# Neighbour attention: values weighed in plain float by halves of 64 columns instead of in high and low parts

## The reference, cut to what matters

```python
s = jnp.concatenate([s_win.reshape(B, NA_HEADS, GRID_W, n_win), s_meta], axis=-1)
p = jax.nn.softmax(s, axis=-1).astype(v.dtype)
p_win = p[..., :n_win].reshape(B, NA_HEADS, GRID_W, win_r, NA_WIN_C)
p_meta = p[..., n_win:]
return (jnp.einsum('bhqrc,brqchd->bqhd', p_win, v_win)
        + jnp.einsum('bhqm,bmhd->bqhd', p_meta, v_meta))
```

## Time and profile before

| | |
|---|---|
| median of 3 runs | 1414.36 us (1412.99 to 1416.44) |
| the profiled execution, its own time | 1412.37 us |
| its span, first to last instruction | 1410.6 us |
| mean granted TensorE clock | 0.982 |
| TensorE / VectorE / ScalarE / GpSimd busy | 1335.9 / 777.8 / 507.1 / 606.6 us |
| the neighbour stage | about 1060 to 1365 us of the span |

### The profile page before, as it was taken

The page is one execution under the profiler, slowest core; times in us unless marked ns, Lnnn a source line. Parts: engine busy times, 40 slices in busy tenths (PEclk is TensorE's granted clock), DMA queues, the critical chain, the costliest instruction groups (busy, mean ns, idle before and its releaser), DMA issues.

```text
span 1410.6 us, 20322 instructions
## 1 busy us (share of the span) xinstructions
PE 1335.9 (95%) x6862; PEld 1076.8 (76%) x6862; DVE 777.8 (55%) x1507; ACT 507.1 (36%) x1066; POOL 606.6 (43%) x367
## 2 busy tenths in 40 slices
PE   7999999998999999999985899999899999999987
PEld 6877777785888888888874677777677888888865
DVE  4237775645556565511142677777425776666761
ACT  3233334213333333200023566666103444444420
POOL 5423332353444444555530444443265555544411
PEclk9999999999999999999997999999899999999999
DMA  6422222232333333333230111111043322222112
GB/s 177 107 66 76 70 65 75 75 90 61 103 89 99 94 89 101 96 102 95 85 105 16 45 46 31 45 30 45 15 130 89 83 68 64 71 71 70 48 33 69
DMA packets 196560, 105.38 MB, mean 75 GB/s; under 512 B 18982, under 2 KB 194444, under 8 KB 196508
## 3 DMA queue, kind: packets, MB, share of 16 engines
q1 hardware_dynamic: 196060, 104.00, 25.8%
q0 software_dynamic: 432, 0.69, 0.3%
q10 hardware_dynamic: 16, 0.00, 0.0%
HBM read 102.57 MB, written 2.10 MB: 74 GB/s over the span
## 4 chain that ended last, share of the span: by engine, by line
PE 81%; DVE 6%; issue 5%; POOL 3%; ACT 3%; DMA 1%; SPq 0%; DVEq 0%; POOLq 0%; ACTq 0%
PE ps L352 19%; PE ps L353 19%; PE ps L354 18%; PE ps L374 9%; PE ps L1237 2%; PE ps L1248 1%; POOL w_low L339 1%; PE ps L1265 1%; PE ps L1267 1%; PE ps L1266 1%; POOL y_low L660 1%; PE ps L898 1%; POOL sq L641 1%; PE ps L920 1%; PE ps L1291 1%
## 5 line engine op out<-in xcount | busy, mean ns | idle before, releaser
L339 POOL TENSOR_TENSOR w_low<-w_raw,w_high 128x1024 fp32r<-128x1024 f32 x183 | 447.8, 2448 | 547.3 <-DVE w_high L334 547.2
L352 PE MATMUL ps<-h_high,w_high 128*128 128x512 f32 x864 | 352.9, 408 | 11.4 <-DVE h_low L475 8.4
L353 PE MATMUL ps<-h_low,w_high 128*128 128x512 f32 x864 | 343.5, 398 | 0.0
L354 PE MATMUL ps<-h_high,w_low 128*128 128x512 f32 x864 | 341.9, 396 | 0.0
L334 DVE CAST w_high<-w_raw 128x1024 fp32r<-128x1024 f32 x183 | 136.9, 749 | 138.0 <-PE ps L354 74.0
L352 PEld LDWEIGHTS ps<-h_high,w_high 128*128 128x128 f32 x864 | 163.3, 189 | 61.6 <-issue 20.5
L354 PEld LDWEIGHTS ps<-h_high,w_low 128*128 128x128 f32 x864 | 163.7, 189 | 37.6
L353 PEld LDWEIGHTS ps<-h_low,w_high 128*128 128x128 f32 x864 | 163.5, 189 | 35.0 <-issue 1.7
L2054 DVE SCALAR_TENSOR_TENSOR z<-ps,cv,z 128x511 f32<-128x511 f32 x44 | 33.0, 750 | 97.8 <-ACT z L1518 97.8
L1518 ACT ACTIVATE z<-ps,cv 128x512 f32<-128x512 f32 x44 | 34.3, 779 | 121.9 <-PE ps L354 121.7
L354 PE MATMUL ps<-m_high,w_low 128*128 128x512 f32 x176 | 69.4, 395 | 0.0
(11 more groups left out here) (338 smaller groups left out, 2508.7 us busy)
## 6 DMA issues: line engine op xcount, KB each, us to landing
w_raw<-in_w_in_dram SPq DMA_DIRECT2D x150, 256.0 KB, 3.2
w_raw<-in_w_up_dram SPq DMA_DIRECT2D x88, 256.0 KB, 3.2
w_raw<-in_w_out_dram SPq DMA_DIRECT2D x44, 256.0 KB, 3.0
w_raw<-in_w_down_dram SPq DMA_DIRECT2D x32, 256.0 KB, 3.0
w_raw<-in_w_down_dram SPq DMA_DIRECT2D x16, 192.0 KB, 2.6
rel<-in_rel_bias_dram SPq DMA_DIRECT2D x8, 384.0 KB, 3.2
x_tok<-in_x_dram SPq DMA_DIRECT2D x4, 512.0 KB, 5.7
w_raw<-in_w_ob_dram SPq DMA_DIRECT2D x8, 256.0 KB, 2.9
```

The source lines that it names most:

```text
L339: pool.tensor_tensor(w_low[:, n % RING, :], w_raw[:, n % RAW, :], w_high[:, n % RING, :].bitcast(F32), ALU.subtract).then_inc(low_made, 1)
L352: pe.matmul(acc, wh, mh, start=first and k == 0, stop=False)
L353: pe.matmul(acc, wh, ml, start=False, stop=False)
L354: done = pe.matmul(acc, wl, mh, start=False, stop=last and k == tiles - 1)
```

## The change

The values and the probabilities of the neighbour stage are kept as plain float (F32) instead of high and low parts. `weigh` does, for each key tile and each head, one plain float matmul with the 64 value columns of that head, which writes 64 of the 128 partitions of bank 4; then one for each head with the 16 meta keys. `turn` transposes the 16 meta columns straight from the probabilities. `probs` divides window and meta columns in one operation per head. `copy_b` is one copy, `gated` one operation with 128 rows. `place_v` on VectorE goes, and ScalarE's second operation in its `place_v` sets the semaphore `nv_ready` that TensorE waits for in its place. ScalarE's `copy_a` writes `np_`; `keep_v` loses its second copy. VectorE's list loses `place_v` in both places. `weigh` waits for ScalarE's copy by name too.

```diff
@@ buffers of the neighbour stage @@
-                nv_high = sb("nv_high", [P, 2, 4, P], F32R, a)
-                nv_low = sb("nv_low", [P, 2, 4, P], F32R, a)
-                nv_meta = sb("nv_meta", [80, 2, P], F32R, a)
-                nvf_meta = sb("nvf_meta", [P, 80], F32, a)
+                nv = sb("nv", [P, 2, 4, P], F32, a)
+                nv_meta = sb("nv_meta", [META, 2, P], F32, a)
...
-                ne_meta = sb("ne_meta", [P, 2, 2, 80], F32, a)
-                np_high = sb("np_high", [P, 3, 2, 2 * P], F32R, a)
-                np_low = sb("np_low", [P, 3, 2, 2 * P], F32R, a)
-                np_meta = sb("np_meta", [80, 2, 2 * P], F32R, a)
+                np_ = sb("np_", [P, 3, 2, 2 * P], F32, a)
+                np_meta = sb("np_meta", [META, 2, 2 * P], F32, a)
@@ GpSimd @@
-            pool.memset(nv_meta[:].bitcast(F32), 0.0).then_inc(s["mv_cleared"], 1)
@@ TensorE: turn @@
                 for h in range(2):
-                    mm = pe.transpose(ps[0:80, 3, (2 + h) * P:(3 + h) * P], ne_meta[:, t % 2, h, :], ident[:])
+                    mm = pe.transpose(ps[0:META, 3, (2 + h) * P:(3 + h) * P],
+                                      ne[:, t % 2, h, NA_META[t]:NA_META[t] + META], ident[:])
@@ TensorE: weigh @@
                 pe.wait_ge(s["t_copied_b"], i * 8 + (4 * c + 2 * p + 2))
+                pe.wait_ge(s["t_copied_a"], i * 8 + (4 * c + 2 * p + 2))
                 if p == 0:
-                    pe.wait_ge(s["nv_low_"], i * 2 + (c + 1))
+                    pe.wait_ge(s["nv_ready"], i * 2 + (c + 1))
...
-                    acc = ps[:, 4, :].rearrange("p (h q) -> p h q", h=2)[:, :, q]
-                    vh, vl = nv_high[:, z_, a + p, :], nv_low[:, z_, a + p, :]
-                    pe.matmul(acc, vh, np_high[:, a, :, q], start=a == p, stop=False)
-                    pe.matmul(acc, vh, np_low[:, a, :, q], start=False, stop=False)
-                    pe.matmul(acc, vl, np_high[:, a, :, q], start=False, stop=False)
-                pe.matmul(ps[:, 4, :], nv_meta[:, z_, :], np_meta[:], start=False, stop=True).then_inc(s["t_summed"], 1)
+                    for h in range(2):
+                        d = slice(h * HD, (h + 1) * HD)
+                        pe.matmul(ps[d, 4, q], nv[:, z_, a + p, d], np_[:, a, h, q], start=a == p, stop=False)
+                for h in range(2):
+                    d = slice(h * HD, (h + 1) * HD)
+                    mm = pe.matmul(ps[d, 4, 0:2 * P], nv_meta[:, z_, d], np_meta[:, h, :], start=False, stop=True)
+                mm.then_inc(s["t_summed"], 1)
@@ TensorE: turn_v @@
-                pe.transpose(ps[0:80, 6, 0:P], nvf_meta[:], ident[:]).then_inc(s["nv_turned"], 1)
+                pe.transpose(ps[0:META, 6, 0:P], nvf[:, 0:META], ident[:]).then_inc(s["nv_turned"], 1)
@@ ScalarE: place_v @@
-                act.activation(nv_high[:, c % 2, :, :], ps[:, 5, :].rearrange("p (a d) -> p a d", d=P), ACT.Copy)
-                for r in (0, 32, 64):
-                    v = act.activation(nv_meta[r:r + META, c % 2, :], ps[r:r + META, 6, 0:P], ACT.Copy)
-                v.then_inc(s["nv_high_"], 1)
+                act.activation(nv[:, c % 2, :, :], ps[:, 5, :].rearrange("p (a d) -> p a d", d=P), ACT.Copy)
+                act.activation(nv_meta[:, c % 2, :], ps[0:META, 6, 0:P], ACT.Copy).then_inc(s["nv_ready"], 1)
@@ VectorE: probs @@
-                    dve.tensor_scalar(ne_meta[:, t % 2, h, :].rearrange("p (r m) -> p r m", m=META),
-                                      five(ne[:, t % 2, h:h + 1, m:m + META]), nm[:, t % 2, 2, h:h + 1], None, ALU.mult)
-                    p = dve.tensor_scalar(ne[:, t % 2, h, k:k + w], ne[:, t % 2, h, k:k + w], nm[:, t % 2, 2, h:h + 1],
+                    p = dve.tensor_scalar(ne[:, t % 2, h, 0:w], ne[:, t % 2, h, 0:w], nm[:, t % 2, 2, h:h + 1],
                                           None, ALU.mult)
@@ VectorE: copy_b @@
-                dve.tensor_copy(np_meta[:, :, q], src).then_inc(s["t_meta"], 1)
-                dve.tensor_tensor(np_low[:, a:a + n, :, q], turned(n), np_high[:, a:a + n, :, q].bitcast(F32), ALU.subtract)
-                dve.wait_ge(s["t_meta"], i * 8 + (4 * c + t + 1))
-                dve.tensor_tensor(np_meta[32:64, :, q], src[32:64], np_meta[32:64, :, q].bitcast(F32), ALU.subtract)\
+                dve.tensor_copy(np_meta[:, :, q], ps[0:META, 3, 2 * P:4 * P].rearrange("p (h q) -> p h q", h=2))\
                     .then_inc(s["t_copied_b"], 1)
@@ VectorE: gated @@
-                for h in range(2):
-                    d = slice(h * HD, (h + 1) * HD)
-                    y = dve.tensor_tensor(ny[d, q], ps[d, 4, h * 2 * P:(h + 1) * 2 * P], ng[d, c % 2, q], ALU.mult)
-                y.then_inc(s["t_y"], 1)
+                dve.tensor_tensor(ny[:, q], ps[:, 4, 0:2 * P], ng[:, c % 2, q], ALU.mult).then_inc(s["t_y"], 1)
```

More of the change, by code:

```diff
@@ L400, in program @@
             om_added rel_in nb_ready
-            q_sq q_kept q_sum q_root q_normed n_high n_low nv_kept nv_turned nv_high_ nv_low_ g_part g_done
-            t_scored t_masked t_neg t_exp t_inv t_probs t_turned t_copied_a t_meta t_copied_b t_summed t_y
+            q_sq q_kept q_sum q_root q_normed n_high n_low nv_kept nv_turned nv_ready g_part g_done
+            t_scored t_masked t_neg t_exp t_inv t_probs t_turned t_copied_a t_copied_b t_summed t_y
             t_high t_low
@@ L1319, in pair @@
                         if t == 0:
-                            pe.wait_ge(s["nv_low_"], 8)
+                            pe.wait_ge(s["nv_ready"], 8)
                             pe.wait_ge(s["t_low"], 6)
@@ L1725, in copy_a @@
                 act.wait_ge(s["t_turned"], i * 8 + (4 * c + t + 1))
-                act.activation(np_high[:, a:a + n, :, t % 2 * P:(t % 2 + 1) * P], turned(n), ACT.Copy)\
+                act.activation(np_[:, a:a + n, :, t % 2 * P:(t % 2 + 1) * P], turned(n), ACT.Copy)\
                     .then_inc(s["t_copied_a"], 1)
@@ L1759, in keep_v @@
                     act.wait_ge(s["nv_turned"], i * 2 + c)
-                act.activation(halves(nvf), wide(5), ACT.Copy)
-                act.activation(nvf_meta[:].rearrange("p (r m) -> p r m", m=META), five(ps[:, 5:6, 0:META]), ACT.Copy)\
-                    .then_inc(s["nv_kept"], 1)
+                act.activation(halves(nvf), wide(5), ACT.Copy).then_inc(s["nv_kept"], 1)
             def gate(i, c):
@@ L1818, in pair @@
                     gate(i, c + 1)
-            act.wait_ge(s["mv_cleared"], 2)
             square(0, 0, 0)
@@ L2265, in probs @@
             def probs(i, c, t):
-                w, k, m = NA_W[t], NA_WIN[t], NA_META[t]
+                w = META + NA_W[t]
                 dve.wait_ge(s["t_exp"], i * 16 + (8 * c + 2 * t + 2))
@@ L2278, in copy_b @@
             def copy_b(i, c, t):
-                n, a = NA_W[t] // P, NA_SLOT[t]
                 q = slice(t % 2 * P, (t % 2 + 1) * P)
                 dve.wait_ge(s["t_copied_a"], i * 8 + (4 * c + t + 1))
-                src = ps[0:80, 3, 2 * P:4 * P].rearrange("p (h q) -> p h q", h=2)
-                dve.tensor_copy(np_meta[:, :, q], src).then_inc(s["t_meta"], 1)
-                dve.tensor_tensor(np_low[:, a:a + n, :, q], turned(n), np_high[:, a:a + n, :, q].bitcast(F32), ALU.subtract)
-                dve.wait_ge(s["t_meta"], i * 8 + (4 * c + t + 1))
-                dve.tensor_tensor(np_meta[32:64, :, q], src[32:64], np_meta[32:64, :, q].bitcast(F32), ALU.subtract)\
+                dve.tensor_copy(np_meta[:, :, q], ps[0:META, 3, 2 * P:4 * P].rearrange("p (h q) -> p h q", h=2))\
                     .then_inc(s["t_copied_b"], 1)
@@ L2323, in gate @@
                 dve.tensor_tensor(ng[:, c % 2, :], ps[:, 7, :], ng[:, c % 2, :], ALU.mult).then_inc(s["g_done"], 1)
[L2325 to L2331, removed]
             def pair(i, c, more=True):
@@ L2362, in pair @@
                 if more:
-                    place_v(i, c + 1)
                     probs(i, c + 1, 0)
@@ L2373, in _ @@
             make_high(dve, N_NA + 6)
-            place_v(0, 0)
             masked(0, 0, 0)
```

## The result

The changed kernel takes 1406.51 us (median of 5 runs, 1404.85 to 1407.8) against 1413.53 for the kernel before (1411.44 to 1416.44) in the same comparison: a ratio of 0.9949 with a 95% interval of [0.9938, 0.9959], 7.0 us less, where 1407.7 and 6.7 less were forecast.

The account below looks back on a forecast made before the run. TensorE, busy 95% of the span, was taken to bound the kernel. Terms summing to -6.7 us took the profiled 1412.37 to 1405.7, plus 2.0 for the median: 1407.7, range 1403 to 1414 (main case 1403.5 to 1410).

Parts of the forecast that it names:

- weighing, the first 15: TensorE's weighing in plain float: a draw, 2.01 or 1.96 us against 1.96; +0.4 us over all 16.
- narrow transposes: Meta transposes shrinking from 80 columns to 16: step stays 0.11 us, so 0; upper bound +4.6, plus 7.9 if one-pass is lost.
- wait for the values' banks: Next pair's key projection waits until the turned values are read; ScalarE alone would release the bank earlier: -4.0 us.
- last turn of a pair: Its start 0.22 us after the value transpose falls to 0.11 as VectorE's probabilities get shorter: -0.8 us.
- probabilities of the last pair: TensorE waits for them twice; two VectorE operations of 0.29 us fewer recover most: -0.9 us.
- wait ahead of the last weighing: TensorE idles 1.47 us at stage end for three VectorE operations; only one of 0.42 stays: -1.0 us.
- Part 1: Pricing of the weighing on TensorE: edges of 0.095 us plus uncovered first weight loads, 0.055 for 64 columns, 0.105 for 128.
- The weakest step: Assumption that 16-column meta transposes cost the same as 80-column ones, 0 us, though no profile row showed a narrow transpose.
- one-pass: Rival: meta transposes stay one-pass but get an edge and small load, +4.6 us, giving 1412.3; chance 0.27.
- two-pass rivals: Rival: meta and value transposes lose the one-pass form, price 12.5 us, giving 1420.2; chance 0.12.
- The rival of uncovered loads: In the weighing, the halves' weight loads don't overlap: 16 loads of 0.055 us each time, 14.1 in all, giving 1421.8; chance 0.01.
- The clock after the stage: Clock granted at 0.51 for 3.3 us after the stage's two last waits; shortening them might gain 1.6 more, not counted.

Follow-up runs that it names:

- e1: Kernel before, with only VectorE's two subtractions placing the next pair's values moved ahead of copy_b of tile 3: 1408.29 us, ratio 0.9963.
- e4: Changed kernel, with the meta keys' value and probability buffers 80 rows high again, extra rows cleared once: 1402.61 us, repeated 1402.32 us.
- e3: Changed kernel, with the weighing's loops exchanged so one half's three window steps precede the other's: 1411.23 us, ratio to the kernel before 0.9988.
- e6: Changed kernel, with VectorE's old load restored by spare operations and values placed on VectorE again, behind copy_b of tile 3: 1408.71 us.

## Why the prediction was right

It was right in its mechanism and in the sign of every term but was 1.6 us short of what the trace shows. That it lies within 0.3 us of the difference of the medians is in part luck: they differ by 7.0 us, and by 7.9 when the changed kernel ran again, while the trace has 8.3 where the change acts. Measured from the stage's own steps:

| term | forecast | measured |
|---|---|---|
| weighing, the first 15 | +0.4 | +0.2: what follows is included, +0.04 before a sum, -0.01 before a transpose |
| narrow transposes | 0 | 0, all steps 0.109 or 0.110 |
| wait for the values' banks | -4.0 | -5.3 (the same in e1) |
| last turn of a pair | -0.8 | -0.6 |
| probabilities of the last pair | -0.9 | -0.6 |
| wait ahead of the last weighing | -1.0 | -1.0 |
| gating at the end | -0.4 | -0.4 |
| last weighing, first to last matmul | not counted apart | -0.3; its edges in and out lie in the waits around it |
| sum | -6.7 | -8.0; the trace has -8.3 |

- **The mis-sized term** is the wait for the banks, 4.0 forecast and 5.3 measured. The 4.0 priced the six waits at line 374 that the earlier trace rows lists, and these were 4.0. It left out two things. The last pair waits for the same banks a seventh time, ahead of its output projection at line 352, 0.61 us over a step. And the first weight load after each wait is uncovered, 0.10 each time and 0.7 in all, though Part 1 had priced just that from the earlier trace rows. TensorE in order of time, the seventh wait in the kernel before:

```profile
1333.33 0.39 PE L354 MATMUL ps<-h_high,w_low 128*128 128x512 f32 x1
1334.17 0.47 PE L352 MATMUL ps<-y_high,w_high 128*128 128x512 f32 x1 [0.45 <-issue]
1334.47 0.39 PE L353 MATMUL ps<-y_low,w_high 128*128 128x512 f32 x1
```

The same place in the changed kernel, where the step is a plain 0.23:

```profile
1331.96 0.39 PE L350 MATMUL ps<-h_high,w_low 128*128 128x512 f32 x1
1332.19 0.39 PE L348 MATMUL ps<-y_high,w_high 128*128 128x512 f32 x1
```

- **The probabilities** were sized too large, twice. The last turn of a pair went from 0.22 to 0.13, not to 0.11. Of the two waits in the last pair the second went, but the first only fell from 0.73 to 0.51.
- **The weighing** came out as priced: two halves side by side, 0.09 to enter, 0.10 for the inner edge, 0.09 to leave. With the load of what follows it takes 2.00 or 1.95, where 2.01 and 1.96 were forecast. e4 took the inner edge away and it gave 2.35, where the low bound of the prediction had 2.4 for it. So the draw holds: seven matmuls of 512 columns and three of 256 at a step of 0.23 and 0.11, against eight in plain float that run two at a time.
- **The weakest step**, that narrow transposes stay at full price and no more, held; the one-pass and the two-pass rivals are both refuted by the steps, 0.109 or 0.110 with one record each. The Trainium skill (TensorEngine Tiling (Array Packing), Restrictions) has column tiling exclude transpose mode for fp32, and the trace agrees with the reading that a transpose of 16 columns isn't tiled in columns.
- **The rival of uncovered loads** is refuted: the window part is 1.24, and 12 uncovered loads of 0.055 would have added 0.66.
- **The clock after the stage** was not counted on, and it stayed halved in the changed kernel though the wait ahead of the last weighing fell from 1.47 to 0.43. So shorter waits alone did not avoid it.
- The 0.3 us that the table leaves are many small differences of steps that I can't assign.
- The forecast for e3 was wrong both ways. The one for e6 (5 to 6 us) was too large against 3.6 in the stage and 2.2 to 2.8 by the medians, for the reasons given there.

## What to carry to other kernels

When a change rewrites the arithmetic of a stage that one engine fills, look first at what that engine waits for: here moving two operations ahead of others in VectorE's list gave 5 of the 7 us and left the arithmetic alone. Price a wait as what sticks out plus the first weight load after it. Small matmuls of an odd shape in a run of others cost 0.15 us of edge each time here; padding them with cleared rows to the neighbours' shape (16 to 80 rows) took it away and made the fastest version here, 1402.6 us.

## What the runs showed of the hardware that I had not expected

- TensorE starts matmuls out of the order of its list when they use the other half of the columns: in each weighing of e3 the seventh record started at 0.488, ahead of the fourth at 0.698, and never earlier. Whether records, matmuls or time set this reach isn't shown. Alternating the halves in the list is still worth 0.48 us per weighing.
- The stretch of half clock right after the stage comes or not with the version and is the same in its repeats (two of the changed kernel with it, two of e4 without), but it follows neither the length of the weighings (e3 with the longest and e4 with the shortest both lack it) nor the waits ahead of it (0.43 and 1.44 us with it in the changed kernel and without it in e3 and e4).
- Edge prices are nearly constant: 0.088 to 0.101 us between the shapes 128 x 128, 128 x 64, 16 x 64 and 64 x 128 (rows x columns of the loaded operand), plus 0.05 for a first load of 64 columns and 0.055 for that of a transpose.
